# Convolution units on VectorE, a two-operation search step on ScalarE, and one written order for the selection

## What is computed

```python
# branch A: each query keeps the 256 keys of highest index score
rel = relu(einsum('bthd,bsd->bths', iq, ik)); score = einsum('bths,bth->bts', rel, iw)
score = where(visible, score, -inf); _, sel = top_k(score, 256)
out = softmax attention over the kept keys, with ALiBi
# branch C: gated input, causal depthwise convolution of width 31, LayerNorm, swish
c = a * sigmoid(g)
y = conv_general_dilated(concat([left, c]), w[:, None, :], feature_group_count=512) + b
y = silu(layer_norm(y, ln_g, ln_b))
```

## Time and profile before

| | us |
|---|---|
| median of three runs (2917.6 to 2918.76) | 2918.38 |
| the profiled execution | 2916.02 |
| its span, first to last instruction | 2914.2 |
| TensorE busy | 2697.1 |
| VectorE busy | 1962.8 |
| ScalarE busy | 1503.0 |
| GpSimd busy | 1315.7 |

### The profile page before, as it was taken

One profiled execution on the slowest core, in us unless ns is written; L12 is line 12 of the kernel. 1 busy time (PEld: TensorE's weight loads), 2 busy tenths in 40 slices (PEclk: granted clock), 3 DMA queues, 4 the chain that ended last, 5 costly groups with the idle time before them and its releaser, 6 DMA issues. The chain is left out here.

```text
span 2914.2 us, 40267 instructions
## 1 busy us (share of the span) xinstructions
PE 2697.1 (93%) x14029; PEld 2488.9 (85%) x14029; DVE 1962.8 (67%) x4027; ACT 1503.0 (52%) x2633; POOL 1315.7 (45%) x939
## 2 busy tenths in 40 slices
PE   6999999899999897948999878899999999999998
PEld 6999999899999897848999756777788998888886
DVE  6477769979896866550463378889976667555554
ACT  5376698788778676735312267677760002111111
POOL 1100387789798666629545354321244332111110
PEclk9999999999999998979999989999999999999999
DMA  4433223333332223212465543221136556121121
GB/s 164 124 124 133 92 82 119 105 121 114 112 121 93 93 73 102 89 59 91 154 195 171 158 123 93 68 59 51 51 117 243 165 167 228 48 71 57 62 71 37
DMA packets 271865, 320.43 MB, mean 110 GB/s; under 512 B 37041, under 2 KB 235185, under 8 KB 271021
## 3 DMA queue, kind: packets, MB, share of 16 engines
q1 hardware_dynamic: 171123, 190.02, 21.2%
q10 hardware_dynamic: 100538, 127.82, 12.4%
HBM read 196.36 MB, written 120.73 MB: 109 GB/s over the span
## 5 line engine op out<-in xcount | busy, mean ns | idle before, releaser
L1640 PE MATMUL psum<-hT_hi,j_whi 128*128 128x416 f32 x2440 | 876.5, 359 | 90.5 <-POOL j_wlo L1449 60.4
L1640 PE MATMUL psum<-hT_hi,j_wlo 128*128 128x416 f32 x2440 | 862.6, 354 | 0.0
L1640 PE MATMUL psum<-hT_lo,j_whi 128*128 128x416 f32 x2440 | 861.5, 353 | 0.0
L1255 POOL TENSOR_TENSOR v_y<-v_y,v_product 128x422 f32<-128x422 f32 x540 | 615.6, 1180 | 43.1 <-ACT v_product L1237 42.9
L1640 PEld LDWEIGHTS psum<-hT_hi,j_whi 128*128 128x128 f32 x2440 | 463.6, 190 | 102.4 <-issue 66.0
L1640 PEld LDWEIGHTS psum<-hT_lo,j_whi 128*128 128x128 f32 x2440 | 464.6, 190 | 9.6 <-issue 1.6
L448 DVE TENSOR_SCALAR_CACHE_REDUCE s_tie<-s_key,s_bits 128x640 bf16<-128x640 f32 (+14 forms) x352 | 464.2, 1319 | 12.3
L1640 PEld LDWEIGHTS psum<-hT_hi,j_wlo 128*128 128x128 f32 x2440 | 462.9, 190 | 6.0
L1237 ACT ACTIVATE v_product<-v_x,v_taps 128x422 f32<-128x422 f32 x600 | 351.7, 639 | 192.4 <-POOL v_y L1255 177.8
L1449 POOL TENSOR_TENSOR j_wlo<-j_w,j_whi 128x1024 fp32r<-128x1024 f32 x61 | 151.3, 2480 | 275.4 <-ACT j_whi L1484 275.3
L1502 ACT ACTIVATE j_out<-psum 128x416 f32<-128x416 f32 x285 | 143.7, 505 | 248.6 <-PE psum L1640 236.2
(11 more groups left out here) (293 smaller groups left out, 4856.4 us busy)
## 6 DMA issues: line engine op xcount, KB each, us to landing
T_dram<-j_out ACTq DMA_DIRECT2D x59, 624.0 KB, 2.9
j_w<-in_w_in ACTq DMA_DIRECT2D x59, 512.0 KB
m_gate<-T_dram SPq DMA_DIRECT2D x60, 416.0 KB, 3.5
T_dram<-j_out ACTq DMA_DIRECT2D x59, 416.0 KB, 2.4
m_oraw<-B_dram SPq DMA_DIRECT2D x15, 832.0 KB, 5.6
M_dram<-m_merged ACTq DMA_DIRECT2D x5, 1664.0 KB, 7.5
n_x<-in_x_prompt SPq DMA_DIRECT2D x16, 512.0 KB, 5.3
f_mraw<-M_dram SPq DMA_DIRECT2D x16, 512.0 KB, 4.6
```

The source lines that it names most:

```text
L1255: pool.tensor_tensor(y[k % 2][:], y[k % 2][:], product[n % RING][:], ALU.add).then_inc(added, 1)
L1640: last = pe.matmul(bank, w[p][:, k, :], h[:, k, t0:t0 + SPAN], start=(k == 0 and q == 0), stop=(k == KD - 1 and q == 2))
```

## The change

Three of the 20 convolution units, (group 0, stretch 2), (1, 2) and (2, 2), become VectorE's own: SyncE loads their two inputs into two buffers of their own, VectorE multiplies them, applies the 31 taps one after the other, and SyncE stores the result. The other 17 are spread over 42 jobs instead of 20 over 43. ScalarE's search step keeps the bits as an integer alone, so that one of three small operations goes, and its sum and sign are held in PSUM (bank 7). The order of the selection, the three units in it, is one written list with due times; VectorE's program, ScalarE's due times and SyncE's queue are read from it. By the new list ScalarE's steps begin at the spans (job, span) (8, 3), (12, 0), (17, 4), (23, 1), (29, 0), (34, 4), (39, 4) and (44, 1), with 7, 5, 6, 5, 4, 5, 6 and 7 steps put behind that one evacuation; before, tile 9 had 7 in one place and the others at most 2.

```diff
-UNITS = 4 * len(CONV_SPANS)
+OWN = [(0, 2), (1, 2), (2, 2)]
+SHARED = [(s, x) for s in range(4) for x in range(len(CONV_SPANS)) if (s, x) not in OWN]
+UNITS = len(SHARED)
...
-CONV_FROM, CONV_JOBS = 9, 43
+CONV_FROM, CONV_JOBS = 9, 42
...
+PLAN = [("offer", 9, 3), ("unit", 0, 24), ("whole", 4, 75), ("offer", 12, 79), ("unit", 1, 100), ("complete", 9, 146), ("whole", 5, 202),
+        ("offer", 13, 206), ("complete", 12, 263), ("whole", 6, 325), ("offer", 14, 329), ("complete", 13, 386), ("whole", 7, 453),
+        ("offer", 15, 457), ("complete", 14, 517), ("whole", DT, 586), ("offer", 11, 589), ("complete", 15, 653), ("whole", 2, 693),
+        ("offer", 10, 697), ("complete", 11, 747), ("whole", 3, 793), ("offer", 8, 796), ("complete", 10, 847), ("unit", 2, 868),
+        ("complete", 8, 932)]
+ACT_TILES = [t for what, t, _ in PLAN if what == "offer"]
+ACT_DUE = [us + 10 + 0.02 * us for what, _, us in PLAN if what == "offer"]
...
-    a_cnt, a_turn, a_value, a_first, a_start = (sb(f"s_a{n}", [P, 1]) for n in ("cnt", "turn", "value", "first", "start"))
+    a_first, a_start, a_bits = sb("s_afirst", [P, 1]), sb("s_astart", [P, 1]), sb("s_abits", [P, 1], I32)
+    a_cnt, a_turn = c.psum[:, 7, 0:1], c.psum[:, 7, 1:2]
+    own_x, own_y = sb("s_ownx", [P, CW_SPAN + LEFT]), sb("s_owny", [P, CW_SPAN + LEFT])
...
+        def load_own(i):
+            s, x = OWN[i]
+            if i:
+                sp.wait_ge(own_moved, 16 * i)
+            c.wait_for_stored(sp, 4 + 2 * s)
+            first = x * CW_SPAN - LEFT
+            for buf, slot in ((own_x, S_GA), (own_y, S_GG)):
+                sp.dma_start(buf[:], c.T_dram[slot + s, :, first:first + CW_SPAN + LEFT]).then_inc(own_full, 16)
+        def move_own(i):
+            s, x = OWN[i]
+            sp.wait_ge(own_done, i + 1)
+            sp.dma_start(c.Y_dram[s, :, x * CW_SPAN:(x + 1) * CW_SPAN], own_y[:, 0:CW_SPAN]).then_inc(own_moved, 16)
         for t, _ in LOADED[:KEYS]:
             load(t)
+        load_own(0)
...
-        for t, us in FINISHED:
+        for what, t, us in PLAN:
+            if what == "offer":
+                continue
             units(SELECT_US + us)
-            if t == FINISHED[-1][0]:
+            if what == "unit":
+                move_own(t)
+                if t + 1 < len(OWN):
+                    load_own(t + 1)
+                continue
+            if t == PLAN[-1][1]:
...
-            return keys_of(ACT_TILES[self.turn]) * 0.00084 + 1.25
+            return keys_of(ACT_TILES[self.turn]) * 0.00084 + 1.0
...
-            do(act.activation(a_junk[:, 0:n], tops, ACT.Sign, scale=a_sign[:, p:p + 1], bias=level, accum_out=a_cnt[:]))
-            do(act.activation(a_turn[:], a_cnt[:], ACT.Sign, bias=a_least[:, p:p + 1]))
+            do(act.activation(a_junk[:, 0:n], tops, ACT.Sign, scale=a_sign[:, p:p + 1], bias=level, accum_out=a_cnt))
+            do(act.activation(a_turn, a_cnt, ACT.Sign, bias=a_least[:, p:p + 1]))
             if b:
-                do(act.activation(a_bits[:], a_turn[:], ACT.Identity, scale=2.0 ** (b + 15), bias=value))
-                self.steps.did(act.activation(a_value[:], a_turn[:], ACT.Identity, scale=2.0 ** (b + 15), bias=value))
+                do(act.activation(a_bits[:], a_turn, ACT.Identity, scale=2.0 ** (b + 15), bias=value))
...
+        def unit(i):
+            s = OWN[i][0]
+            tap = lambda k: c.parT[:, s, k:k + 1]
+            if i == 0:
+                c.wait_for_parameters(vec)
+            vec.wait_ge(own_full, 32 * (i + 1))
+            do(vec.tensor_tensor(own_x[:], own_x[:], own_y[:], ALU.mult))
+            y = own_y[:, 0:CW_SPAN]
+            do(vec.tensor_scalar(y, own_x[:, 0:CW_SPAN], tap(0), tap(CONV), ALU.mult, ALU.add))
+            for k in range(1, CONV):
+                ins = vec.scalar_tensor_tensor(out=y, in0=own_x[:, k:k + CW_SPAN], scalar=tap(k), in1=y, op0=ALU.mult, op1=ALU.add)
+                if k < CONV - 1:
+                    do(ins)
+            ins.then_inc(own_done, 1)
...
-        offer(0)
-        whole(DVE_TILES[0])
-        for x in range(len(ACT_TILES) - 1):
-            offer(x + 1)
-            complete(x)
-            if x + 1 < len(DVE_TILES):
-                whole(DVE_TILES[x + 1])
-        complete(len(ACT_TILES) - 1)
+        for what, t, _ in PLAN:
+            if what == "offer":
+                offer(ACT_TILES.index(t))
...
```

More of the change, by code:

```diff
@@ L277 @@
 LIFT = 1
-ACT_TILES = [9, 12, 13, 14, 15, 11, 10, 8]
-DVE_TILES = [4, 5, 6, 7, DT, 2, 3]
-LOADED = [(9, 0), (4, 1), (12, 2), (5, 1), (13, 0), (6, 1), (14, 2), (7, 1), (15, 0), (DT, 1), (11, 2), (2, 1), (10, 0), (3, 1), (8, 2)]
-def select_times():
-    us, due, done = 0.0, [], []
-    def spend(t, columns, steps):
-        nonlocal us
-        us += 0.00104 * columns * keys_of(t) + 0.74 * steps
-    def offer(t):
-        spend(t, 1, 2.4)
-        due.append(us + 12 + 0.02 * us)
-    def finish(t, bits):
-        spend(t, bits + 7.8, bits + 1.4)
-        done.append((t, us))
-    offer(ACT_TILES[0])
-    finish(DVE_TILES[0], 32)
-    for x, t in enumerate(ACT_TILES[1:]):
-        offer(t)
-        finish(ACT_TILES[x], 16)
-        if x + 1 < len(DVE_TILES):
-            finish(DVE_TILES[x + 1], 32)
-    finish(ACT_TILES[-1], 16)
-    return due, done
-ACT_DUE, FINISHED = select_times()
+PLAN = [("offer", 9, 3), ("unit", 0, 24), ("whole", 4, 75), ("offer", 12, 79), ("unit", 1, 100), ("complete", 9, 146), ("whole", 5, 202),
[5 more added lines that the diff above has]
+ACT_DUE = [us + 10 + 0.02 * us for what, _, us in PLAN if what == "offer"]
+LOADED = [(9, 0), (4, 1), (12, 2), (5, 1), (13, 0), (6, 1), (14, 2), (7, 1), (15, 0), (DT, 1), (11, 2), (2, 1), (10, 0), (3, 1), (8, 2)]
 KEYS = 3
@@ L344, in stage_select @@
     a_least = sb("s_aleast", [P, 2])
+    own_x, own_y = sb("s_ownx", [P, CW_SPAN + LEFT]), sb("s_owny", [P, CW_SPAN + LEFT])
     c.after_select = sb.at
     S = c.sem
+    own_full, own_done, own_moved = S("s_own_full"), S("s_own_done"), S("s_own_moved")
     own_steps, act_steps = S("s_steps"), S("s_act_steps")
@@ L425, in step @@
             tops = key[slot[t]][:].bitcast(BF16)[:, 1:2 * n:2]
-            level, value = (a_bits[:].bitcast(F32), a_value[:]) if b < 14 else (a_first[:], a_start[:])
+            level, value = (a_bits[:].bitcast(F32), a_bits[:]) if b < 14 else (a_first[:], a_start[:])
             if b == 14:
@@ L429, in step @@
                 act.wait_ge(ready, self.turn + 1)
[L430 to L431 removed]
+            do(act.activation(a_junk[:, 0:n], tops, ACT.Sign, scale=a_sign[:, p:p + 1], bias=level, accum_out=a_cnt))
+            do(act.activation(a_turn, a_cnt, ACT.Sign, bias=a_least[:, p:p + 1]))
             if b:
[L433 to L434 removed]
+                do(act.activation(a_bits[:], a_turn, ACT.Identity, scale=2.0 ** (b + 15), bias=value))
                 self.bit -= 1
             else:
[L437 removed]
+                act.activation(a_found[p][:], a_turn, ACT.Identity, scale=2.0 ** 15, bias=value).then_inc(found, 1)
                 self.turn, self.bit = self.turn + 1, 14
@@ L505, in vector @@
         without_search(1)
-        offer(0)
-        whole(DVE_TILES[0])
-        for x in range(len(ACT_TILES) - 1):
-            offer(x + 1)
-            complete(x)
-            if x + 1 < len(DVE_TILES):
-                whole(DVE_TILES[x + 1])
-        complete(len(ACT_TILES) - 1)
+        for what, t, _ in PLAN:
+            if what == "offer":
+                offer(ACT_TILES.index(t))
+            elif what == "complete":
+                complete(ACT_TILES.index(t))
+            elif what == "whole":
+                whole(t)
+            else:
+                unit(t)
     def wait_for_selected(eng):
         eng.wait_ge(early_stored, 32)
+        eng.wait_ge(own_moved, 16 * len(OWN))
         for k in range(KEYS):
@@ L1172, in load @@
     def load(sp, u):
-        s, x = u // 5, u % 5
+        s, x = SHARED[u]
         if u == 0:
@@ L1286, in stage_convolve @@
     c.load_unit, c.move_unit = load, move
+    c.wait_for_parameters = lambda eng: eng.wait_ge(par_ready, 2)
     c.wait_for_moved = lambda eng: eng.wait_ge(unit_moved, UNITS)
```

2 lines of the change are left out of this document (removed).

## The result

| kernel | median us | lowest to highest | against before, 95% interval |
|---|---|---|---|
| before | 2917.99 | 2917.39 to 2918.76 | |
| changed | 2804.01 | 2801.79 to 2806.39 | 0.9609 [0.9593, 0.9626] |

The kernel before has one run more here than in the table ahead of the prediction. The change takes 114 us off, 3.9%. The forecast was 2827, with 2798 to 2862 as its range. The profiled execution of the changed kernel took 2803.79 us with a span of 2802.0; its span is 112.2 us shorter than that of before.

The account below looks back on a forecast made before the run. TensorE, 93% busy, was held by six stops blamed on SyncE's queue order: 2914.2 - 117.5 + 16 + 7 + 3 = 2822.7; with 1.8 outside the span and the median 2.4 higher, 2827 us, range 2798 to 2862.

Parts of the forecast that it names:

- The 117.5 us: TensorE's six long projection stops: 100.6 us idle plus 17 of slow clock, all won back by the new queue order.
- Unit 0: 22 us: VectorE's first convolution unit, run before GpSimd's first tap: 31 two-input operations of 0.66 us, 22 us in all.
- Units 1 and 2: 47 us: VectorE's units beside busy GpSimd: 22 us of operations plus 25 of GpSimd's adds each, ends 22 and 61.
- the forecast's pause: In unit 1, a pause in which ScalarE makes no products for GpSimd's adds, leaving 24 adds, 25 us.
- the second and third rival: VectorE's units: port makes them 61 us or more, 2863, chance 0.2; every operation waits 9.7 us, 3317, chance 0.05.
- First stop: +16: TensorE at 537 us: six ScalarE steps on tile 13 delay the first key-and-value load; +16 us, 8 to 31.
- Unit 2 and the burst of seven: +7: At 1125 us seven ScalarE steps precede VectorE's unit 2, while GpSimd falls behind; +7 us, 0 to 23.
- The four spans of cover: At the burst of seven, ScalarE's evacuations can be four spans late, 18 us, against 15 us behind.
- Other bursts: +3: Five other ScalarE bursts of 11 to 14 us, with cover and mostly a free GpSimd; +3 us, 0 to 8.
- The step: ScalarE's search step without one small operation, sums and signs in PSUM: 0.2 plus 0.08 us less a step.
- ScalarE isn't the bound: this is worth nothing of its own: ScalarE's shorter search step saves time there, but hides under the matmuls and gains nothing alone.
- The first rival: Nothing new stops TensorE: VectorE's units run as listed and the load lands in time; 2801 us, chance 0.17.

Follow-up runs that it names:

- the reverse edit: Changed kernel with SyncE's queue made from 0.86 of VectorE's due times, except the last tile's; 2935.61 us, ratio 1.0077.
- moving the burst: Changed kernel with ScalarE's first step on tile 13 due 9 us later, so six steps stand behind the first key-and-value load; 2798.25 us.
- the charge alone: Kernel before, old three-operation step kept, with the planner charging ScalarE's step 1.0 us instead of 1.25 beyond the columns; 2829.6 us, ratio 0.9702.

## Why the prediction was right, and where its sizes were off

- **The 117.5 us.** Right: the jobs of before show 116.7, and the reverse edit brings such stops back. The condition given, that VectorE is nowhere more than 35 us late, held: its latest tile, tile 9, is done at 459.8 us, 11 behind its due time in the list, and GpSimd has no wait for the queue over 3.5 us. But the list wasn't the only part that could do it, as the step's bullet below says.
- **Unit 0: 22 us.** It took 23.4, its operations 0.66.
- **Units 1 and 2: 47 us.** They took 39.9 and 38.7. I took a stretch to last for the sum of both engines' work, a whole add of 1.06 us for each that came in between; an operation beside GpSimd's adds loses 0.72. During ScalarE's burst eight operations ran at 0.66, as the forecast's pause had it. The ends of 22 and 61 hold it, and the 9.7 us of the second and third rival came to no two-input operation; the longest took 2.69.
- **First stop: +16.** It measured 6.7 (its own two terms, 13.7 and 3, make 16.7 and not 16), and this is the term that was most mis-sized, in two places. Tile 13 was offered at 518.3 us, not 532: 7 us by the shorter unit 1, and 8 because the plain operation that had taken 9.70 us took 1.59 this time, less 1 for the longer unit 0. The second of these is luck: no part of the change aims at it. So the burst didn't wait for the offer; it began when ScalarE's order came to it, at 523.7. Six steps took 15.2 us, for 15.6. The load landed 2.3 us behind its issue, for 3. With an offer that early, the forecast's own sum gives 523.7 + 15.6 + 3 = 542.3 and a stop of 5.4; it was 5.09. The mechanism held, and moving the burst proved it.
- **Unit 2 and the burst of seven: +7.** Nothing: no job from 26 to 49 takes over 22.9 us. The four spans of cover were enough. This is the other half of the miss.
- **Other bursts: +3.** One stop of 2.15 us, 2.3 in its job. It doesn't stand behind a burst: ahead of it ScalarE makes single steps behind the evacuations (at 693.0 and 697.2 us) and six taps. So the size was near and the place wasn't the one named.
- **The step.** Small operations in PSUM take less than I gave them. Groups by shape in the changed kernel, 400 to 1350 us, against 295 ns each before:

```profile
L432 ACT ACTIVATE psum<-psum,s_aleast 128x1 f32<-128x1 f32 x103 | 24.3, 236 | 3.3
...
L434 ACT ACTIVATE s_abits<-psum,s_abits 128x1 int32<-128x1 f32 x90 | 23.5, 261 | 2.9
```

  With the accumulator's read at 152 ns for 188, the step on 1792 columns is 2.54 us long for 2.85, 0.31 less, for a forecast of 0.28.
- **"ScalarE isn't the bound: this is worth nothing of its own".** Wrong in general, and right only beside the list. I priced the edit by the instruction's time and passed over the planner's charge that changes with it. That number alone is worth 86 us in the kernel before. It is also the answer to a question that the prediction left: why VectorE waited 188.9 us for ScalarE's half. I had read that wait as a fact of the stage; half of it was written into ScalarE's order by the charge (95.0 us are left with the charge alone), and with the list 11.0 are left.
- **Sum.** 2914.2 - 116.7 + 9.0 = 2806.5, and 2802.0 was measured; 1.3 us of the rest are small excesses that other jobs had before, and 3 lie behind job 60, where executions of one kernel differ by as much. The forecast of 2827 was 23 us too high: 9.3 from the first stop, 7 from the burst of seven, 0.7 from the others, 4.5 from this rest, and 2.2 from the median, which I had put 2.4 us above the profiled run and which lies 0.2 above; 0.8 goes the other way, for the six stops. The first rival, nothing new at 2801, was the nearest, and I gave it 0.17 because a burst stood right ahead of the load; the burst cost 6.7 and no more.

What would show it, point by point: no stop over 15 us, the one at 537 just under the 6 that I gave as its least (5.09), no GpSimd wait for the queue over 15 us, operations of 0.66 and of 1.38, the last tile done at 1228.0 and its store issued at 1236.5 for 1230, and VectorE's waits at 11 for under 60.

## What to carry to other kernels

Where several streams share one queue in written order, look first for the stream whose due times aren't kept: moving its entries behind the loads that others need gave 108 us here with not one operation added, taken away or changed. When an edit makes an operation cheaper, look at every planner number that follows it, since its place in an order can be worth many times its length (86 us against 10). And when parts remove the same stops, test each alone, since what one is worth beside the others (0 to 5 us) tells nothing of its worth without them (97).

## What was not expected of the hardware

- Two-input VectorE operations on 422 columns beside GpSimd's adds take 1.38 us, and the adds 1.42, in place of 0.66 and 1.06: VectorE loses 0.72 us at each, GpSimd 0.36, and the two together are done in less than the sum of their lengths. With one of the two inputs in PSUM both are back at their own length.
- The plain operation of unit 1, one input in SBUF, takes 1.16 us beside GpSimd and 0.50 alone. Writing to PSUM it takes 0.72 in either place, so it is slower alone and faster beside GpSimd.
- A plain VectorE operation can wait through a whole row of GpSimd's instructions, not only one. In the kernel with the charge alone, timelines of VectorE and then GpSimd:

```profile
525.20 12.63 DVE L463 TENSOR_SCALAR s_tie<-s_key,s_bits 128x1664 bf16<-128x1664 f32 x1
...
525.02 2.42 POOL L1449 TENSOR_TENSOR j_wlo<-j_w,j_whi 128x1024 fp32r<-128x1024 f32 x1
...
527.37 9.58 POOL L1255 TENSOR_TENSOR v_y<-v_y,v_product 128x422 f32<-128x422 f32 x9
```

  The operation ends when GpSimd's ten instructions without a gap do, at 537; elsewhere in the same trace it takes 0.6 to 2.2 us. An operation of this line of 7.5 to 13.3 us stands in eight of the fourteen traces, at other tiles each time, and none in the changed kernel (3.27 at most). That is part of why VectorE came earlier there than forecast, and it hangs on how the two engines happen to meet.
- A ScalarE operation on one column takes 236 ns from PSUM to PSUM, 261 from PSUM to SBUF and 295 within SBUF.
